# A two-layer decoder step in fp32 halves on one Trainium2 core: the prompt in token blocks, a Newton step in the norms, and the moved group weights of layer B's decode

## The reference, cut to what matters

```python
def layer_norm(x, g, b):
    mu = jnp.mean(xf, -1, keepdims=True)
    var = jnp.mean(jnp.square(xf - mu), -1, keepdims=True)
    y = (xf - mu) * lax.rsqrt(var + LN_EPS) * g + b
...
for i in range(DEPTH):                       # DEPTH = 2
    x = post_norm(x, 0.5 * swiglu(x, ...), i, 0)
    x = post_norm(x, mixer_a(x) if i % 2 == 0 else mixer_b(x), i, 1)
    x = post_norm(x, 0.5 * swiglu(x, ...), i, 2)
# post_norm(x, d) = layer_norm(ALPHA * x + d)
# mixer_b: three groups (window, dilation) = (128, 1), (512, 4), (2048, 16),
#          outputs combined by softmax over the groups' log denominators
# decode: for each of 8 sequences, group and head, 129 gathered rows of a
#         cache of up to 2048 rows of keys and values; the shifted caches are outputs too
```

## Time and profile before

| what | value |
|---|---|
| three runs | 2849.19, 2843.28, 2849.41 us, median 2849.19 |
| profiled execution | 2846.3 us, of it the span of the trace 2844.2 us |
| granted TensorE clock, mean | 0.983 |
| PE | 2721.6 us busy, 96% of the span |
| PEld, DVE, ACT, POOL | 91%, 37%, 28%, 24% |
| DMA | 478.99 MB, mean 168 GB/s; in the busiest slice of the 40, 377 GB/s |

### The profile page before, as it was taken

The page is one execution under the profiler, slowest core; times in us unless marked ns, Lnnn a source line. Parts: engine busy times, 40 slices in busy tenths (PEclk is TensorE's granted clock), DMA queues, the critical chain, the costliest instruction groups (busy, mean ns, idle before and its releaser), DMA issues. The chain is left out here.

```text
span 2844.2 us, 55401 instructions
## 1 busy us (share of the span) xinstructions
PE 2721.6 (96%) x22548; PEld 2600.8 (91%) x22548; DVE 1062.3 (37%) x1705; ACT 805.1 (28%) x1568; POOL 680.1 (24%) x717
## 2 busy tenths in 40 slices
PE   7999998989999998999998999999998898999998
PEld 6999998768999998999998899889986668999997
DVE  2222225566222225222235423444354445422224
ACT  3222212453222213222222422434242223222222
POOL 2222321114222232222321112111222113222231
PEclk9999999999999999999999999999999999999999
DMA  7777743214666644666632134222428994566641
GB/s 241 242 245 232 204 120 88 59 29 139 218 220 217 203 153 155 219 209 209 207 112 77 53 102 124 68 79 58 125 90 323 357 377 128 200 218 208 229 153 46
DMA packets 460502, 478.99 MB, mean 168 GB/s; under 512 B 55886, under 2 KB 433951, under 8 KB 456120
## 3 DMA queue, kind: packets, MB, share of 16 engines
q1 hardware_dynamic: 454880, 464.85, 49.5%
q0 software_dynamic: 5392, 11.67, 1.4%
q10 hardware_dynamic: 64, 0.08, 0.0%
HBM read 463.55 MB, written 198.59 MB: 233 GB/s over the span
## 5 line engine op out<-in xcount | busy, mean ns | idle before, releaser
L758 PE MATMUL bank<-sb_xh,sb_wl 128*128 128x272 f32 x4368 | 944.0, 293 | 48.5 <-DVE sb_wl L1539 26.7
L762 PE MATMUL bank<-sb_xh,sb_wh 128*128 128x272 f32 x4368 | 935.5, 291 | 0.0
L760 PE MATMUL bank<-sb_xl,sb_wh 128*128 128x272 f32 x4368 | 932.0, 290 | 0.0
L1539 DVE TENSOR_TENSOR sb_wl<-sb_raw,sb_wh 128x1024 fp32r<-128x1024 f32 (+1 forms) x337 | 471.5, 1399 | 915.1 <-ACT sb_wh L1262 906.7
L758 PEld LDWEIGHTS bank<-sb_xh,sb_wl 128*128 128x128 f32 x4368 | 705.4, 191 | 55.5 <-DVE sb_wl L1539 29.6
L760 PEld LDWEIGHTS bank<-sb_xl,sb_wh 128*128 128x128 f32 x4368 | 705.5, 191 | 0.6
L762 PEld LDWEIGHTS bank<-sb_xh,sb_wh 128*128 128x128 f32 x4368 | 700.9, 191 | 0.0
L1262 ACT CAST sb_wh<-sb_raw 128x1024 fp32r<-128x1024 f32 (+1 forms) x337 | 374.3, 1112 | 938.5 <-PE bank L762 916.7
L758 PE MATMUL bank<-sb_hh,sb_wl 128*128 128x272 f32 x1408 | 309.3, 291 | 0.0
L1969 POOL CAST sb_hh<-sb_h 128x544 f32 x88 | 130.3, 1481 | 745.2 <-DVE sb_h L1553 745.2
L760 PE MATMUL bank<-sb_hl,sb_wh 128*128 128x272 f32 x1408 | 304.7, 287 | 0.0
(11 more groups left out here) (271 smaller groups left out, 2318.7 us busy)
## 6 DMA issues: line engine op xcount, KB each, us to landing
out_state_b_s<-in_cache_b_kv SPq DMA_DIRECT2D x176, 704.0 KB, 6.2
sb_raw<-in_ffn_w_gate SPq DMA_DIRECT2D x88, 512.0 KB, 4.0
sb_raw<-in_ffn_w_up SPq DMA_DIRECT2D x88, 512.0 KB, 4.6
sb_raw<-in_ffn_w_down SPq DMA_DIRECT2D x64, 704.0 KB, 4.8
sb_raw<-in_attn_b_w_qkv SPq DMA_DIRECT2D x72, 512.0 KB, 3.8
sb_dkvb<-in_cache_b_kv SPq DMA_DIRECT2D x72, 512.0 KB, 10.8
out_state_b_s<-in_cache_b_kv SPq DMA_DIRECT2D x32, 1016.0 KB, 7.6
sb_raw<-in_cache_b_kv SPq DMA_DIRECT2D x48, 512.0 KB, 10.2
```

The lines of the kernel that those rows point to most:

```text
L758: pe.matmul(acc(s, h), third(hl, k) if slot == 2 else wl[slot][:, k, :], hi(k)[:, halves[h]], start=start and k == 0, stop=False)
L760: pe.matmul(acc(s, h), third(hh, k) if slot == 2 else wh[slot][:, k, :], lo(k)[:, halves[h]], start=False, stop=False)
L762: last = pe.matmul(acc(s, h), third(hh, k) if slot == 2 else wh[slot][:, k, :], hi(k)[:, halves[h]], start=False, stop=end)
L1539: dve.tensor_tensor(wl[j % 2][:, 0:ph.chunks, :], raw[j][:, 0:ph.chunks, :], v.bitcast(F32), ALU.subtract).then_inc(wl_rdy, 1)
```

## The change

Three parts; the whole program moves by some lines, so a line of before has another number after.

1. **Start.** The prompt comes by four transfers, one for each block of 128 tokens, each with its own semaphore; the samples have a fifth. PE transposes block by block into pairs of banks (the bias lines go to banks 4 to 6 instead of 0 to 2), the samples last. ACT copies a block's first four chunks from its bank to `z` and, a second time, to `xh`, DVE copies the other four chunks to `z`, ACT casts those to `xh`, and DVE makes two subtractions over four chunks each. The first weight split stands behind block 1. SP's loop over the first phase's weights is opened up: four weight loads, then the copies of the caches, then the wait for the bias lines.
2. **Norm.** DVE's reciprocal and ACT's square root are replaced: ACT takes Abs_reciprocal_sqrt of the variance and its square, and DVE's new `refine` makes one Newton step of two operations from them, r = y (1.5 - 0.5 v y y). `scale` waits for it. In the first half `refine` stands behind the four deviations, in the second behind the first.
3. **Layer B's rounds.** `last_round(n)` is called behind the last `keep_keys` and ahead of `own_heads`.

```diff
@@ SP
-            sp.dma_start(xin[:], t["x_prompt"][0].rearrange("(b p) d -> p b d", p=P)).then_inc(in_ld, 16)
-            sp.dma_start(xsin[:], t["x_sample"].rearrange("n t d -> (n t) d")).then_inc(in_ld, 16)
+            for b in range(NBLK):
+                sp.dma_start(xin[:, b, :], t["x_prompt"][0, b * P:(b + 1) * P, :]).then_inc(in_ld[b], 16)
+            sp.dma_start(xsin[:], t["x_sample"].rearrange("n t d -> (n t) d")).then_inc(in_ld[NBLK], 16)
...
+                elif ph is up[0, 0]:
+                    load_first(ph)
+                    for j in range(RAW):
+                        keep(ph, 0, j)
+                    keep_window(ph.ffn, 0, LINE_ROWS)
+                    sp.wait_ge(line_o, 32)
+                    repeat_lines(0, LINE_ROWS)
+                    load_units(ph, 1)
@@ PE
-            pe.wait_ge(in_ld, 32)
...
+            for b in range(NBLK):
+                pe.wait_ge(in_ld[b], 16)
+                if b == 2:
+                    pe.wait_ge(line_c, 1)
+                for c in range(KC):
+                    mm = pe.transpose(bank[X_BANKS[b][c // 4]][:, (c % 4) * P:(c % 4 + 1) * P], xin[:, b, c * P:(c + 1) * P], ident[:])
+                    if c % 4 == 3:
+                        mm.then_inc(init_t, 1)
...
@@ ACT
-                act.wait_ge(ln_rs, 2 * (2 * n + h) + 2)
-                act.activation(rstd[:, halves[h]], rstd[:, halves[h]], ACT.Sqrt).then_inc(ln_root, 1)
+                act.wait_ge(ln_rs, 2 * (2 * n + h) + 1)
+                act.activation(sqb[1][:, halves[h]], rstd[:, halves[h]], ACT.Abs_reciprocal_sqrt).then_inc(ln_est, 1)
+                act.wait_ge(ln_est, 2 * n + h + 1)
+                act.activation(sqb[0][:, halves[h]], sqb[1][:, halves[h]], ACT.Square).then_inc(ln_root, 1)
...
+            def first_x(b):
+                cols, src = slice(b * P, (b + 1) * P), bank[X_BANKS[b][0]][:].rearrange("p (c n) -> p c n", n=P)
+                act.wait_ge(init_t, 2 * b + 1)
+                act.copy(z[:, 0:4, cols], src).then_inc(ln_aff, 1)
+                act.copy(xh[:, 0:4, cols], src).then_inc(x_hi, 1)
+                act.wait_ge(x_cp, b + 1)
+                act.copy(xh[:, 4:8, cols], z[:, 4:8, cols]).then_inc(x_hi, 1)
...
+            first_x(0)
+            first_x(1)
             split(phases[0], 0, 0, 0)
+            first_x(2)
+            first_x(3)
+            first_samples()
             split(phases[0], 1, 1, 0)
@@ DVE
-                dve.wait_ge(ln_rs, 2 * (2 * n + h) + 1)
-                dve.reciprocal(r, r).then_inc(ln_rs, 1)
+            def refine(n, h):
+                r = rstd[:, halves[h]]
+                dve.wait_ge(ln_root, 2 * n + h + 1)
+                dve.scalar_tensor_tensor(r, r, -0.5, sqb[0][:, halves[h]], ALU.mult, ALU.mult).then_inc(ln_rs, 1)
+                dve.wait_ge(ln_rs, 2 * (2 * n + h) + 2)
+                dve.scalar_tensor_tensor(r, r, 1.5, sqb[1][:, halves[h]], ALU.add, ALU.mult).then_inc(ln_newt, 1)
...
-                    dve.wait_ge(ln_root, 2 * n + h + 1)
+                    dve.wait_ge(ln_newt, 2 * n + h + 1)
...
+                refine(n, 0)
                 scale(n, 0, 0)
...
                     deviate(n, 1, q)
+                    if q == 0:
+                        refine(n, 1)
                     scale(n, 1, q)
...
+            def first_x(b):
+                cols = slice(b * P, (b + 1) * P)
+                dve.wait_ge(init_t, 2 * b + 2)
+                dve.tensor_copy(z[:, 4:8, cols], bank[X_BANKS[b][1]][:].rearrange("p (c n) -> p c n", n=P)).then_inc(x_cp, 1)
+                dve.wait_ge(ln_aff, b + 1)
+                for q in range(2):
+                    dve.wait_ge(x_hi, 2 * b + q + 1)
+                    v = slice(4 * q, 4 * q + 4)
+                    ins = dve.tensor_tensor(xl[:, v, cols], z[:, v, cols], xh[:, v, cols].bitcast(F32), ALU.subtract)
+                    if b == 2:
+                        ins.then_inc(x_lo[0], 4)
...
-                    if layer:
-                        last_round(n)
                     if G > 1:
...
+                        last_round(n)
                         if 0 < n <= NS:
                             own_heads(n - 1)
```

More of the change, by code:

```diff
@@ L1355, in project, with first_samples @@
                     affine(n, 1, q, not nxt)
-            def high(k, c):
-                act.wait_ge(ln_aff, KC * k + c + 1)
-                act.copy(xh[:, c, :], z[:, c, :]).then_inc(x_hi, 1)
+            def first_x(b):
[5 more added lines that the diff above has]
+                act.copy(xh[:, 4:8, cols], z[:, 4:8, cols]).then_inc(x_hi, 1)
+            def first_samples():
+                act.wait_ge(init_t, 2 * NBLK + 1)
+                src = bank[3][:, 0:KC * SAMPLE].rearrange("p (c n) -> p c n", n=SAMPLE)
+                act.copy(z[:, :, SEQ:TOK], src).then_inc(ln_aff, 1)
+                act.copy(xh[:, :, SEQ:TOK], src).then_inc(x_hi, 1)
             def run(ph):
@@ L1499, in _ @@
             act.dma_start(dec_lines_d, lin2[:]).then_inc(line_o, 16)
-            for c in range(KC):
-                act.wait_ge(init_t, c + 1)
-                act.copy(z[:, c, 0:SEQ], bank[c % 4][:])
-                act.copy(z[:, c, SEQ:TOK], bank[4 + c % 4][:, 0:SAMPLE]).then_inc(ln_aff, 1)
-                high(0, c)
+            first_x(0)
+            first_x(1)
             split(phases[0], 0, 0, 0)
+            first_x(2)
+            first_x(3)
+            first_samples()
             split(phases[0], 1, 1, 0)
@@ L1643, in project, with first_samples @@
                     split_third(nxt)
[L1645 to L1648 removed]
+            def first_x(b):
[9 more added lines that the diff above has]
+                        ins.then_inc(x_lo[0], 4)
+            def first_samples():
+                dve.wait_ge(x_hi, 2 * NBLK + 1)
+                dve.tensor_tensor(xl[:, :, SEQ:TOK], z[:, :, SEQ:TOK], xh[:, :, SEQ:TOK].bitcast(F32), ALU.subtract).then_inc(x_lo[1], KC)
             def run(ph):
@@ L1884, in _ @@
             dve.wait_ge(line_t, 1)
-            dve.tensor_copy(lin1[:, 0:512], bank[0][0:HEADS, :])
-            dve.tensor_copy(lin1[:, 512:LINES], bank[1][0:HEADS, 0:LINES - 512])
-            dve.tensor_copy(lin2[:], bank[2][0:HEADS, 0:ND]).then_inc(line_c, 2)
-            for c in range(KC):
-                low_first(c)
+            dve.tensor_copy(lin1[:, 0:512], bank[4][0:HEADS, :])
+            dve.tensor_copy(lin1[:, 512:LINES], bank[5][0:HEADS, 0:LINES - 512])
+            dve.tensor_copy(lin2[:], bank[6][0:HEADS, 0:ND]).then_inc(line_c, 2)
+            first_x(0)
+            first_x(1)
             split(phases[0], 0, 0, 0)
+            first_x(2)
+            first_x(3)
+            first_samples()
             split(phases[0], 1, 1, 0)
```

31 lines of the change are left out of this document (15 added, 16 removed).

## The result

The change made the kernel faster: a median of 2823.02 us in 4 runs against 2848.47 in 4 of the kernel before, a ratio of 0.9914 with a 95% interval of 0.9897 to 0.9931. The forecast was 2823.5 with a range of 2812 to 2834.

A forecast was written before the change was run, and what follows sets the result against it. PE works nearly all the time, so only its waits and lower-clock time can be won: start 6.0, norms 9.5, layer B's rounds 8.7, together 24.2 us off 2846.3 or 2849.19, forecast 2823.5, range 2812 to 2834.

The forecast's parts named there:

- The cost of nothing for SyncE's order: Start: loading the first four weights ahead of the cache copies costs nothing; at worst 1.3 us could be lost.
- cold stretch: Start: PE's 27 matmuls in 6.2 us, the pace taken to give 5.5 us for the first unit's 24 matmuls.
- the forecast's upper bound: Start: if the clock rises earlier relative to the products, up to 1.4 us come on top, 7.4 in all.
- The 0.65 more in the norms before a qkv phase: Two norms before a qkv phase: PE is later than DVE by 0.65 us, so about 2.2 us each can be kept.
- the forecast's 2.55: Norms: PE resumes 2.55 us earlier at the low pair behind the second spread, 0.8 + 1.75; not all stays.
- The forecast's step by which only DVE's own gain counts in the second half: Three norms before an up phase: PE catches up with DVE, so only 1.6 us a norm count, 0.8 a half.
- the upper bound of 13.8: Norms: 2.55 us kept in each of five norms and 1.0 in the last, 13.8 us in all.
- the second paragraph of that part: Layer B's rounds: the transfer ring is late next; rounds taken at 24.3 us, six 145.8, 8.7 us less.
- the rival of 26.1 us a round: Layer B's rounds: each gets a DMA wait and half-clock spell; decode loses 2.1 us, total 2834; chance 0.12.
- rounds over 25 us: Layer B's rounds: listed sign that the forecast is wrong; the sign for right was six rounds of 23.5 to 24.6 us.
- The fear that DVE's moved work would be 0.8 us late in two or three rounds: Layer B's rounds: 2.67 us of moved work fit DVE's idle time but for 0.8, delaying the next maximum and key copies.
- The rule against it: Layer B's rounds: at about 358 GB/s from HBM a round could not be under 26.4 us; the sum would end at 2836.

The follow-up runs named there:

- narrow tiles: The whole change, but from the thirteenth tile on layer B's ring takes 768 of 1024 columns on all 128 rows; 2813.64 us, ratio 0.9888 to the kernel before.

## Why the prediction was right

The forecast was 24.2 us less; the medians give 25.4 and the traces 25.9 and 22.0.

**The start.** Forecast 20.3 for the first product and 6.0 us; it was 19.96 and 6.2. The working held: ACT from the end of its table load, DVE as the longer of the two, the split of the first weights in between, block 2's first low half last. The cost of nothing for SyncE's order was right too (20.00 at the start, and no difference in time clear of the noise without it). Behind the first product the clock moved the lead both ways. The "cold stretch" of the earlier trace rows shows 1.00 in the clock column, but its pace is that of the lower level: 27 products in 6.13 us, where the next window (32.4 to 36.0) has 30 in 3.60. After the change that stretch was shorter (14 products in 3.14 us from 19.9 to 23.1, at 0.50), and the lead rose from 6.3 at the first product to 7.3, as the forecast's upper bound had it. The second split then cost PE 0.32 us, and a spell at 0.50 of 6.8 us from 36.75, where before had one of 3.4 from 46.01, took the rest. That 6.2 came so near to 6.0 is luck in part; the first product's place is not.

**The norms.** Forecast 9.5, measured 10.4 by the lead (8.7 by the medians of the part alone). DVE's chain from the first variance to the second took 14.48 us before (1089.09 to 1103.57) and takes 13.69 (1077.92 to 1091.61), 0.79 less; from the second variance to the start of the last four low halves it took 10.95 and takes 10.05 (1091.61 to 1101.66), 0.90 less. Two times 0.8 had been forecast, and the norms before an up phase gained just that sum, 1.69 by DVE's chain and 1.70 by the lead. The 0.65 more in the norms before a qkv phase is not shown: at the first of them kernels with the old norms gain 0.7 of the 2.4 too, and at the second the two traces of the whole change give 2.66 and 1.17. ACT's extra pass cost nothing in the first half: it ends near 1080.1 (its second pass of 0.43 began at 1079.66), and DVE's deviations end at 1080.9. In the second half the two are close, 1093.0 and 1093.4.

One thing the forecast did not have. Before, PE was at the lower clock for 3.4 us behind the wait of 3.73 us: 27 products in 4.93 us from 1106.2 at a mean granted clock of 0.66. Now 30 go in 4.09 us behind the wait of 1.93, at 1.00. PE thus gained about 1.5 us more than the forecast's 2.55 in that place, for a while 4.1 in all, and gave back everything beyond DVE's 1.7 in the three waits of 0.80, 0.65 and 0.65. This is why the total of these waits rose while the norm got shorter: the bound moved from PE behind a wait to DVE's chain. The forecast's step by which only DVE's own gain counts in the second half covered it, and it is what kept the norms from the upper bound of 13.8.

**The rounds.** Forecast 145.8 us for six rounds, measured 146.0. The ring became the bound, as the second paragraph of that part put it, by waits of 1.57, 1.94 and 1.53 us in every second round; none of them brought the lower clock, so the rival of 26.1 us a round, which needed a half-clock spell with each wait, did not come. By its own list the forecast named rounds over 25 us as a sign against it; two are at 25.1 and 25.4, and it is the mean of 24.3 that was right. Of the 8.5 us, 7.4 are left at 2360 of the kernel before: 0.6 more were won ahead of the rounds, and 1.6 went behind them, where a last ring wait of 1.10 us stands and the mean clock is 0.79 over 24.3 us instead of 0.85 over 22.4. The fear that DVE's moved work would be 0.8 us late in two or three rounds shows in no wait of PE in the whole change's rounds; with the ring relieved by narrow tiles it is there, at 0.42 us in two rounds.

**The rule against it.** The forecast set a rule of the Trainium skill, the 358 GB/s of DMA: Bandwidth & Descriptors, section Specifications, against the 408 of the earlier trace rows. Going by the row was right: the rounds now hold 406 to 408 GB/s in every second round. The same page of the Trainium skill, section "Measured (HBM→SBUF, 128 partitions, SWDGE, issued from GpSimd)", itself keeps the 358 for two cores that stream at once. The trace agrees with that reading: one core ran here, at 406 to 408.

**What was not forecast:** 1.8 us in the attentions, where the two traces differ in waits and half-clock spells. No part of the change explains them: the second trace of the whole change loses 0.9 us there, and the kernels with one part alone lose 1.5 to 3.0. Luck of this kind is larger than the error of the whole forecast (0.5 us), so the closeness of the sum says less than the closeness of its terms.

## What to carry to other kernels

Where an engine waits, ask first whose chain the stretch hangs on: the norms before an up phase gained what DVE's chain lost, not what PE's wait lost, and reordering DVE's queue so that what PE needs comes first won another 0.8 us a norm at no work. When a wait is removed in front of a transfer ring, forecast the round by the ring's time per tile; and when fewer bytes are to test that, check the rate, since a tile with fewer rows moved slower than a whole one. Gains under 4 us are better read from a product-by-product comparison of traces than from medians, stretch by stretch, because waits elsewhere move by as much; a second trace of the same kernel tells which stretches can be trusted.
